# Rotary partners by small DMAs inside SBUF in place of a product on TensorE

## The reference

```python
def partial_rope(x, positions, rot_dim):
    half = rot_dim // 2
    inv_freq = jnp.power(jnp.float32(ROPE_THETA), -jnp.arange(half, dtype=jnp.float32) / half)
    ang = positions.astype(jnp.float32)[..., None] * inv_freq
    cos = jnp.cos(ang)[:, :, None, :]
    sin = jnp.sin(ang)[:, :, None, :]
    x1 = x[..., :half].astype(jnp.float32)
    x2 = x[..., half:rot_dim].astype(jnp.float32)
    rot = jnp.concatenate([x1 * cos - x2 * sin, x2 * cos + x1 * sin], axis=-1)
    return jnp.concatenate([rot.astype(x.dtype), x[..., rot_dim:]], axis=-1)
```

```python
    dq = partial_rope(dq.reshape(B_, S, DSA_HEADS, HEAD_DIM), positions, ROPE_DIM_2)
    dk = partial_rope(dk.reshape(B_, S, 1, HEAD_DIM), positions, ROPE_DIM_2)[:, :, 0]
    iq = partial_rope(iq.reshape(B_, S, IDX_HEADS, IDX_DIM), positions, IDX_ROPE_DIM)
    ik = partial_rope(ik.reshape(B_, S, 1, IDX_DIM), positions, IDX_ROPE_DIM)[:, :, 0]
```

## Time and profile before

| what | value |
|---|---|
| time, median of 3 runs | 3048.58 us (3047.69 to 3049.86) |
| the profiled execution's own time | 3042.06 us |
| its span in the trace | 3040.2 us |
| busy: TensorE / DVE / ACT / POOL | 94% / 54% / 41% / 19% of the span |
| mean granted TensorE clock | 0.977 of full speed |
| DMA | 244.35 MB, mean 80 GB/s |

### The profile page before, as it was taken

The page is one execution under the profiler, slowest core; times in us unless marked ns, Lnnn a source line. Parts: engine busy times, 40 slices in busy tenths (PEclk is TensorE's granted clock), DMA queues, the critical chain, the costliest instruction groups (busy, mean ns, idle before and its releaser), DMA issues.

```text
span 3040.2 us, 38912 instructions
## 1 busy us (share of the span) xinstructions
PE 2858.9 (94%) x15604; PEld 2371.1 (78%) x15608; DVE 1643.0 (54%) x2509; ACT 1260.2 (41%) x2104; POOL 571.0 (19%) x435
## 2 busy tenths in 40 slices
PE   8988999999979999999999979999799899799997
PEld 7778999998767888886667758888666678588885
DVE  5785644455875744546846353333558664443334
ACT  5673322234763422225445343333344544343333
POOL 2342000011341000002334140000423342400003
PEclk9999999999989999999999989999899999899998
DMA  4111232232112333231133123332211222122221
GB/s 140 45 43 63 91 92 89 91 98 67 44 36 79 98 97 97 86 105 53 60 101 104 45 66 97 97 97 91 72 62 57 94 98 70 56 85 95 97 94 60
DMA packets 71923, 244.35 MB, mean 80 GB/s; under 512 B 9152, under 2 KB 10816, under 8 KB 71744
## 3 DMA queue, kind: packets, MB, share of 16 engines
q1 hardware_dynamic: 66528, 235.50, 24.1%
q10 hardware_dynamic: 5216, 6.36, 0.6%
HBM read 239.73 MB, written 2.10 MB: 80 GB/s over the span
## 4 chain that ended last, share of the span: by engine, by line
PE 78%; DVE 11%; issue 4%; ACT 4%; POOL 3%; DMA 0%; ACTq 0%; DVEq 0%; POOLq 0%
PE psum L511 21%; PE psum L517 21%; PE psum L514 21%; PE psum L536 2%; PE psum L568 2%; PE psum L562 2%; PE psum L564 1%; DVE temp L1915 1%; DVE weights_hi_lo L1487 1%; DVE small L1913 1%; PE psum L914 1%; PE psum L926 1%; ACT weights_hi_lo L998 1%; PE psum L760 1%; POOL temp L2216 1%
## 5 line engine op out<-in xcount | busy, mean ns | idle before, releaser
L511 PE MATMUL psum<-act_hi_lo,weights_hi_lo 128*128 128x512 f32 (+2 forms) x2640 | 822.0, 349 | 17.5 <-ACT act_hi_lo L1384 15.0
L514 PE MATMUL psum<-act_hi_lo,weights_hi_lo 128*128 128x512 f32 (+2 forms) x2640 | 798.0, 340 | 1.9 <-DVE weights_hi_lo L1487 1.9
L517 PE MATMUL psum<-act_hi_lo,weights_hi_lo 128*128 128x512 f32 (+2 forms) x2640 | 796.6, 339 | 0.3
L1487 DVE TENSOR_TENSOR weights_hi_lo<-weights_float,weights_hi_lo 128x1024 fp32r<-128x1024 f32 (+2 forms) x446 | 572.0, 1283 | 263.5 <-ACT weights_hi_lo L998 262.1
L998 ACT ACTIVATE weights_hi_lo<-weights_float 128x1024 fp32r<-128x1024 f32 (+2 forms) x446 | 463.7, 1041 | 507.8 <-PE psum L517 435.3
L511 PEld LDWEIGHTS psum<-act_hi_lo,weights_hi_lo 128*128 128x128 f32 x2640 | 461.2, 190 | 83.2 <-issue 25.2
L511 PE MATMUL psum<-hidden_hi_lo,weights_hi_lo 128*128 128x512 f32 (+1 forms) x1488 | 501.3, 363 | 12.0 <-ACT hidden_hi_lo L1168 7.3
L517 PEld LDWEIGHTS psum<-act_hi_lo,weights_hi_lo 128*128 128x128 f32 x2640 | 458.5, 189 | 58.8 <-DVE act_hi_lo L2007 1.7
L514 PEld LDWEIGHTS psum<-act_hi_lo,weights_hi_lo 128*128 128x128 f32 x2640 | 459.5, 190 | 57.1 <-issue 3.1
L517 PE MATMUL psum<-hidden_hi_lo,weights_hi_lo 128*128 128x512 f32 (+1 forms) x1488 | 493.1, 358 | 1.7 <-POOL hidden_hi_lo L1744 1.2
L514 PE MATMUL psum<-hidden_hi_lo,weights_hi_lo 128*128 128x512 f32 (+1 forms) x1488 | 492.5, 357 | 0.6 <-DVE weights_hi_lo L1487 0.6
(11 more groups left out here) (246 smaller groups left out, 3304.3 us busy)
## 6 DMA issues: line engine op xcount, KB each, us to landing
weights_float<-in_w_ff SPq DMA_DIRECT2D x128, 512.0 KB, 3.5
weights_float<-in_w_gu SPq DMA_DIRECT2D x88, 512.0 KB, 3.4
weights_float<-in_w_in SPq DMA_DIRECT2D x70, 512.0 KB, 3.4
weights_float<-in_w_down SPq DMA_DIRECT2D x32, 448.0 KB, 3.3
weights_float<-in_w_out SPq DMA_DIRECT2D x16, 512.0 KB, 3.4
weights_float<-in_w_down SPq DMA_DIRECT2D x16, 512.0 KB, 3.5
weights_float<-in_w_mv SPq DMA_DIRECT2D x16, 512.0 KB, 3.2
weights_float<-in_w_mix SPq DMA_DIRECT2D x16, 512.0 KB, 3.2
```

Source lines behind the costliest of these rows:

```text
L511: e.matmul(slot[:, place:place + c1 - c0], w_hi[:, col], x_hi[:, c0:c1], start=first, stop=False)
L514: e.matmul(slot[:, place:place + c1 - c0], w_lo[:, col], x_hi[:, c0:c1], start=False, stop=False)
L517: mm = e.matmul(slot[:, place:place + c1 - c0], w_hi[:, col], x_lo[:, c0:c1], start=False, stop=final)
L1487: e.tensor_tensor(lo[:, 0:cols], K.staged(n)[:, 0:cols], hi[:, 0:cols].bitcast(F32), ALU.subtract).then_inc(*K.did("lo", n))
```

## The change

The rotation products on TensorE and their matrices go. ACT issues small DMAs that copy each rotating half of a head's rows from the tile to the place of its partner in `rot1` or `rot2`, all inside SBUF: four DMAs of 8 rows for a tile of two heads, eight of 4 rows for a tile of four heads. The sign of the first half goes into the table of sines, by negative frequencies. DVE multiplies the partner rows by the sines in place. In block 1 ACT issues them three steps after the tile's statistics; in block 2 two steps after the tile's end, where the product was, and DVE's two operations stand two steps later than before. As the partner buffer is one, each group of DMAs waits until the tile before is rotated. `ORDER2` starts with ik in place of the two iq tiles. DVE fills `rot1` with zeros once, at the start.

```diff
-ORDER2 = ([("iq", 0), ("iq", 1), ("ik", 0)] + [(kind, n) for n in range(3) for kind in ("cq", "ck")]
+ORDER2 = ([("ik", 0), ("iq", 0), ("iq", 1)] + [(kind, n) for n in range(3) for kind in ("cq", "ck")]
...
+def partners(e, K, dst, src, head, half, mark):
+
+    for at in range(0, P, head):
+        for to, of in ((at, at + half), (at + half, at)):
+            e.dma_start(dst[to:to + half, :], src[of:of + half, :]).then_inc(
+                *(K.did("partner", *mark, by=16) if to == P - head + half else K.did("partner_row", *mark, to, by=16)))
...
 def tensor_attention(e, w, K, B, l):
-        if s in ROT_AT1:
-            kind, n = ROT_AT1[s]
-            B.clear(*d)
-            w.wait_ge(*done("normed", l, kind, n))
-            sums(e, D, m["consts"][:, C_ROT16:C_ROT16 + P], K.raw1[kind == "q"], T1).then_inc(*did("rot", l, kind, n))
-            B.emptied(d, ("sin", l, kind, n))
...
 def tensor_mixers(e, w, K, B, l):
-        if s in ROT_AT2:
-            kind, n = ROT_AT2[s]
-            at = C_ROT16 if kind in ("dq", "dk") else C_ROT8
-            B.clear(2)
-            w.wait_ge(*done("tile", l, kind, n))
-            e.matmul(K.bank[2], m["consts"][:, at:at + P], K.raw2[AT2[kind, n] % 2][:, 0:T2], start=True,
-                     stop=True).then_inc(*did("rot2", l, kind, n))
-            B.emptied((2,), ("sin2", l, kind, n))
...
 def scalar_attention(e, w, K, l):
+        if s - 3 in STAT_AT1:
+            kind, n = STAT_AT1[s - 3]
+            w.wait_ge(*done("normed", l, kind, n))
+            at = TURNS1.index((kind, n))
+            w.wait_ge(*(done("rotated", l, *TURNS1[at - 1]) if at > 0 else done("lam_sums", l)))
+            partners(e, K, K.rot1, K.raw1[kind == "q"], HEAD_DIM, 8, (1, l, kind, n))
...
 def scalar_mixers(e, w, K, l):
+        if s in ROT_AT2:
+            kind, n = ROT_AT2[s]
+            head = HEAD_DIM if kind in ("dq", "dk") else IDX_DIM
+            w.wait_ge(*done("tile", l, kind, n))
+            at = TURNS2.index((kind, n))
+            w.wait_ge(*(done("rotated2", l, *TURNS2[at - 1]) if at > 0 else done("root", "f", DEPTH - 1) if l == 0
+                        else done("sq_stat", "w_ff2", l - 1)))
+            partners(e, K, K.rot2[:, 0:T2], K.raw2[AT2[kind, n] % 2][:, 0:T2], head, head // 8, (2, l, kind, n))
...
 def small_before(e, w, K, l):
+    if l == 0:
+        e.memset(K.rot1, 0.0).then_inc(*did("small", "clean"))
+        w.wait_ge(*done("small", "clean"))
...
 def vector_attention(e, w, K, l):
-            w.wait_ge(*done("rot", l, kind, n))
-            e.tensor_tensor(along(K.rot1, T1), D_, along(m["rope"][:, 1, :], T1), ALU.mult).then_inc(*did("sin", l, kind, n))
+            w.wait_ge(*done("partner", 1, l, kind, n))
+            e.tensor_tensor(K.rot1, K.rot1, m["rope"][:, 1, :], ALU.mult).then_inc(*did("sin", l, kind, n))
...
 def vector_mixers(e, w, K, l):
-        if s - 1 in ROT_AT2:
-            kind, n = ROT_AT2[s - 1]
+        if s - 3 in ROT_AT2:
+            kind, n = ROT_AT2[s - 3]
...
-        if s in ROT_AT2:
-            kind, n = ROT_AT2[s]
-            table = 0 if kind in ("dq", "dk") else 2
-            w.wait_ge(*done("rot2", l, kind, n))
-            w.wait_ge(*last("rotated"))
-            e.tensor_tensor(K.rot2[:, 0:T2], K.bank[2], m["rope"][:, table + 1, 0:T2], ALU.mult).then_inc(
+        if s - 2 in ROT_AT2:
+            kind, n = ROT_AT2[s - 2]
+            table = 1 if kind in ("dq", "dk") else 3
+            w.wait_ge(*done("partner", 2, l, kind, n))
+            e.tensor_tensor(K.rot2[:, 0:T2], K.rot2[:, 0:T2], m["rope"][:, table, 0:T2], ALU.mult).then_inc(
                 *did("sin2", l, kind, n))
...
 def constants():
-                col[p] = freq[d % half]
+                col[p] = -freq[d] if d < half else freq[d - half]
```

More of the change, by code:

```diff
@@ L64 @@
 INADMISSIBLE = -float(2.0 ** 126)
-C_IDENT, C_BLOCK, C_ROT16, C_ROT8, C_INV = 0, 128, 256, 384, 512
-C_CAUSAL, C_CHUNK = 514, 642
-C_COS1, C_SIN1 = 770, 770 + T1
-C_COLS = 770 + 2 * T1
+C_IDENT, C_BLOCK, C_INV = 0, 128, 256
+C_CAUSAL, C_CHUNK = 258, 386
+C_COS1, C_SIN1 = 514, 514 + T1
+C_COLS = 514 + 2 * T1
 PARAMS1 = [("mix_g", DC), ("q_g", 1), ("k_g", 1), ("subln_g", 1), ("conv_w", 16), ("conv_b", 4),
@@ L99 @@
     neg=("neg2", "negx"), max_score=("max_score0", "max_score2", "max_scorex"), rates=("rates2", "ratex", "lam_rate"),
-    scaled=("scaled1", "scaledx"), rotated=("rotated2",), rot=("rot2",), cos=("cos2",), sin=("sin2",),
+    scaled=("scaled1", "scaledx"), rotated=("rotated2",), partner=("partner_row",), cos=("cos2",), sin=("sin2",),
     root=("qk_root", "sub_root", "rec_root", "ln_root"),
@@ L308 @@
 ROT_AT2 = {END2[tile] + 2: tile for tile in ORDER2 if tile[0] in ROPE2}
-ROPE_BEFORE = {("iq", 0): None, ("iq", 1): None, ("ik", 0): ("iq", 0), ("dk", 0): ("iq", 1), ("dq", 0): ("ik", 0),
+ROPE_BEFORE = {("ik", 0): None, ("iq", 0): None, ("iq", 1): ("ik", 0), ("dk", 0): ("iq", 0), ("dq", 0): ("iq", 1),
                ("dq", 1): ("dk", 0), ("dq", 2): ("dq", 0)}
+TURNS1 = sorted(ROT1, key=lambda tile: ROT1[tile])
+TURNS2 = [tile for tile in ORDER2 if tile[0] in ROPE2]
 MEM_LOAD = [60, 76, 90, 60]
@@ L1262, in scalar_mixers @@
                 if ROPE_BEFORE[kind, n] is not None:
-                    w.wait_ge(*done("rot2", l, *ROPE_BEFORE[kind, n]))
+                    w.wait_ge(*done("partner", 2, l, *ROPE_BEFORE[kind, n]))
                     w.wait_ge(*done("cos2", l, *ROPE_BEFORE[kind, n]))
@@ L1724, in vector_attention @@
                 if n > 0:
-                    w.wait_ge(*done("rot", l, kind, n - 1))
+                    w.wait_ge(*done("partner", 1, l, kind, n - 1))
                     w.wait_ge(*done("cos", l, kind, n - 1))
@@ L1732, in vector_attention @@
                     dst = K.raw1[0]
-                    w.wait_ge(*done("rot", l, "k", HEADS - 1))
+                    w.wait_ge(*done("partner", 1, l, "k", HEADS - 1))
                     w.wait_ge(*done("cos", l, "k", HEADS - 1))
@@ L2352, in constants @@
     c[:, C_BLOCK:C_BLOCK + P] = np.kron(np.eye(2), np.ones((HEAD_DIM, HEAD_DIM)))
-    def partner(head, half):
-        r = np.zeros((P, P))
-        for p in range(P):
-            d = p % head
-            if d < half:
-                r[p + half, p] = -1.0
-            elif d < 2 * half:
-                r[p - half, p] = 1.0
-        return r
-    c[:, C_ROT16:C_ROT16 + P] = partner(HEAD_DIM, 8)
-    c[:, C_ROT8:C_ROT8 + P] = partner(IDX_DIM, 4)
     q, k = np.arange(P)[:, None], np.arange(P)[None, :]
```

## The result

The changed kernel takes 3052.13 us, median of 12 runs (3047.51 to 3057.03), beside 3045.40 us of the kernel before (12 runs, 3039.69 to 3050.62): ratio 1.0024, 95% interval [1.0015, 1.0033]. 3052.1 lies inside the range and near its upper end.

The account below looks back on a forecast made before the run. TensorE, busy 94% of the span, was taken as the bound. Gains of 3.0 us in block 1 and 6.6 in block 2, together 9.6, off the 3048.6 median gave 3039.0 us; range 3026 to 3055.

Parts of the forecast that it names:

- The size of an issue: Every partner DMA on ACT: 0.45 us an issue, ends 0.33 and 0.67, so four hold ACT 1.8 us and eight 3.6.
- the prediction's own sum for the index tiles: Block 2, iq and ik: bursts, landings and rotations through one rot2; index product at 1378.1, before 1378.74, 0.6 us gained.
- a rival of 0.03: Low clock once in each attention stage costs 4.7 us, 9.4 together, leaving 3048.4 us; chance 0.03.
- the decision point that I gave: Block 2 index tiles: the slow chain decides once its extra passes 4.8 us per layer.
- slower by the chain: Rival: issues of 0.67 us, landings of 3.8 make the rot2 chain 6.8 us late per layer; 3055.8 us; chance 0.18.
- the waits for the square behind the bursts: Block 1, first three tiles: bursts delay ACT's squares, q0's by 1.1 us; TensorE ends 0.5 us behind.
- DVE never late for a landing: Block 1: landing costs nothing; the tightest tile, q0, has 3.8 us of cover against 2.3.
- The later tiles: Block 1 from q1: bursts fall where ACT waits anyway; from +0.5 to a gain of 1.5 us per layer.
- The gain of 7.2 us of products a layer: Block 1: products removed are worth 7.2 us per layer, of which 1.5 us were forecast as gained.
- DVE holds: Rival: TensorE's gains in block 1 and beside the top-k end in waits for DVE; 3047.2 us; chance 0.18.
- dk and dq: Block 2: removed products give 0.9 us for dk and 2.6 for dq per layer, less 0.8 for dq2's addition.
- Its item for dq2's addition: Block 2: the addition, moved directly before the maximum, makes DVE wait for the scores; 0.8 us lost per layer.

Follow-up runs that it names:

- e8: Changed kernel plus eight series of eight DMA issues on ACT behind its last store; an issue takes 0.59 to 0.63 us from SBUF, 0.32 or 0.45 from DRAM.
- e5: Changed kernel, ACT still issuing, with iq0 and iq1 given rot2 buffers and semaphores of their own; ratio 0.9986 to the kernel before.
- e9: Changed kernel plus products nobody reads in front of TensorE's waits at four places; ratio 0.9998 to the kernel before.
- e4: Changed kernel with SyncE, not ACT, issuing the partner DMAs between its weight loads; ratio 0.9994 to the kernel before.
- e2: The change in block 2 alone, block 1 making its rotation products as before; ratio 1.0021 to the kernel before.
- e10: Changed kernel with SyncE issuing, own rot2 buffers for index tiles, and block 1's rotation products kept but unread; ratio 0.9954 to the kernel before.
- e12: Kernel before plus the same unread products at the same four places as e9; ratio 1.0021 to the kernel before.
- e13: Changed kernel, ACT issuing, with block 1's rotation products kept but unread; ratio 1.0049 to the kernel before.

## Why the prediction was wrong

**The size of an issue, the first step that failed.** The bounds were 0.33 and 0.67, taken was 0.45; it is 0.63. The nearest row was a load from DRAM, and e8 shows that the source decides. With 0.63 and landings of 1.7 us (the mean of 1.8, 2.0 and 1.3) behind the burst in place of 2.3, the prediction's own sum for the index tiles gives 24 x 0.18 - 3 x 0.6 = 2.5 us more: +1.9 a layer in place of -0.6. Measured at TensorE: the product at 1381.20 stood at 1375.12 in the kernel before, and the stage began 4.03 us late, so 2.05 us of loss by then. That the two agree so well is in part luck. The prediction's sum ends at the product of the fifth head (1378.74 before), behind the rotation of the third tile. TensorE was stopped one product earlier, by relus that stood on ACT behind the third burst, and the fifth head's product, at 1387.22, waited for nothing:

```profile
1387.22 0.70 PE L813 MATMUL psum<-arena 32*128 32x256 f32 x4
```

The mechanism holds, a chain of bursts through one buffer; e5 shows it by cutting it.

**The clock, which the sum put at nothing.** The stretch then ends at +4.5, not +2. TensorE was busy for 5.3 of the 6.8 us at the lower level, and up to half of that, 2.6 us, is lost: an estimate that closes the gap. The prediction had the clock as a rival of 0.03, apart from the others, and priced a stretch of 10 us at 4.7, idle time included; half of its 5.77 busy us would have been 2.9. Here it isn't a rival but a surcharge: each wait that the change makes or lengthens can bring it. The Trainium skill's page TensorE: Matmul & The Clock Gate (HAM oscillation — how this bites in real kernels) describes this, a wait between batches after which the next ones start at the lower clock; e9 agrees, with 23 us less at the lower level and 7 to 8 us less time. By the decision point that I gave, 0.65 us an issue or 0.52 with landings of 3.3, the chain should not have turned the sign. With the surcharge it turned at 0.63 and 1.7, so the rival "slower by the chain" was the right case. That its +7.2 us is also the time measured is luck: it had 6.8 us a layer from issues of 0.67 and landings of 3.8, where 4.5 were measured with the clock in them, and it had block 1 gaining.

**Block 1.** Named right: the waits for the square behind the bursts, 2.70 and 2.40 us after 0.76 and 0.80 us, DVE never late for a landing. Mis-sized: TensorE is 3 us behind after three tiles, not 0.5. The fall at 72 us can have taken up to 1.7 of that, half of its 3.4 us, and the longer bursts (3.25, 2.61, 2.62 us in place of 1.8) the rest; no run parts the two. The later tiles gave back what was forecast, 2 us. Then a longer wait for ACT at 204.47 and the fall of the clock behind it took that. First the kernel before, then the changed one:

```profile
201.75 1.08 PE L615 MATMUL psum<-arena 64*16 64x512 f32 x8 [0.88 <-ACT temp L1099]
```

```profile
204.47 1.08 PE L626 MATMUL psum<-arena 64*16 64x512 f32 x8 [2.14 <-ACT temp L1102]
```

ACT's issues alone don't make this wait: with SyncE issuing it is still 1.99 us (e4). With block 1 as it was before it is 0.88 (e2), with the products kept but unread beside SyncE's DMAs 1.65 (e10). What part of the change makes it no run settles, and the prediction's sum had no such item. The gain of 7.2 us of products a layer was bound to be small in any case: with ACT free of issues it is 0.6 and 1.9 us (e4). Layer 1 ends level, +0.2. For block 1 the rival "DVE holds", with no gain there, came closest.

**dk and dq.** Right: -2.7 forecast, -2.5 and -2.3 measured. Its item for dq2's addition was not: 0.8 us for DVE is 0.9 us on the lag, but TensorE waits 4.02 us there in place of 0.28, and the third stretch at the lower level stands behind that; in e9, with the wait filled, it is gone.

**What would show it.** I had named issues far from 0.45 as the sign of failure, and that is what came. The clock before 210 us had been named too: it fell at 72 and 205 us. DVE's waits at iq and ik, forecast at 2 to 4 us, were 4.66 to 5.18.

## What to carry to other kernels

Work taken from the engine that bounds a stage is a gain only while nothing new makes that engine wait: price the new wait with what the clock takes behind it, and remember that products at a wait may keep the clock up. They paid in e9 and cost nothing in e10, but they cost 5 to 8 us in e12 and e13, so try them and don't count on them. A transfer through one shared buffer is a chain of issue, landing and use; cut it with a second buffer before tuning its parts. Price a DMA by a row with the same kind of source and target, and if there is none, measure one first.

## What had not been expected of the hardware

An issue with a source in SBUF takes 0.59 to 0.63 us on ACT, for 4 rows as for 128, and 0.62 on SyncE (4 and 8 rows); from DRAM 0.32 us (8 rows) and 0.45 (128). With eight in a row the issues, 5.0 us, outweigh the 1.3 to 2.0 us behind them. The Trainium skill's page DMA: Bandwidth & Descriptors (Why a DMA increments its semaphore by 16 and not by 1) has a transfer of few rows use few engines, which I had let lean the price to the dear side; no run shows a cost of it, as 4 rows are the cheapest of the SBUF series. The same page (Rules for kernel authors) says that spreading DMAs over issuing engines gives no bandwidth and saves sequencer time only; e4 agrees on the second half: an issue is 0.62 us on SyncE too, and taking that time off ACT was worth 8 to 9 us; no run here tests the bandwidth. Whether the first burst of a kernel is always dearer (0.81 us an issue at 68 us) no run was made to show.
